# Hybrid conv/mLSTM step with a mixture of experts: the order of work at the first three expert slots

## The reference, cut to what matters

```python
gp = softmax(x @ w_rg + b_rg); gsel = argmax(gp)              # one group of 4
ep = softmax((x @ w_re + b_re)[group gsel]); top 2 of 4       # two experts in the group
combine = gp_sel * top2 / sum(top2)                           # weight of a token for an expert
g = x @ w_e_gate[e]; u = x @ w_e_up[e]                        # 1024 -> 256 each, 16 experts
act = silu(g) * u * combine[:, e]
out += act @ w_e_down[e]                                      # 256 -> 1024
x = x + gate2 * out; y = rms_norm(x)
```

## Time and profile before

| | |
|---|---|
| time, median of 3 runs | 734.84 us (733.2, 734.84, 737.28) |
| profiled execution, its time | 736.13 us |
| profiled execution, its span | 734.3 us |
| PE busy | 702.0 us (96%) |
| DVE busy | 542.5 us (74%) |
| ACT busy | 345.4 us (47%) |
| POOL busy | 212.8 us (29%) |
| moved by DMA | 149.10 MB |

### The profile page before, as it was taken

One profiled execution on the slowest core, in us unless ns is written; L12 is line 12 of the kernel. 1 busy time (PEld: TensorE's weight loads), 2 busy tenths in 40 slices (PEclk: granted clock), 3 DMA queues, 4 the chain that ended last, 5 costly groups with the idle time before them and its releaser, 6 DMA issues.

```text
span 734.3 us, 11162 instructions
## 1 busy us (share of the span) xinstructions
PE 702.0 (96%) x4432; PEld 612.8 (83%) x4432; DVE 542.5 (74%) x782; ACT 345.4 (47%) x457; POOL 212.8 (29%) x89
## 2 busy tenths in 40 slices
PE   5899999999999999999999999999889999998985
PEld 2499999999898898999999999887358888887863
DVE  3547999999858765865465574556599999988977
ACT  4552223432423443555276031124468888787634
POOL 4004321322200000000000000000129999989476
PEclk9999999999999999999999999999689999999998
DMA  9954145545624356441232534264958999989875
GB/s 332 375 163 143 59 173 173 173 173 174 206 92 77 66 122 128 44 133 58 62 118 75 162 115 144 114 258 162 420 182 335 398 402 409 416 326 398 312 252 197
DMA packets 75607, 149.10 MB, mean 203 GB/s; under 512 B 11302, under 2 KB 54626, under 8 KB 68836
## 3 DMA queue, kind: packets, MB, share of 16 engines
q1 hardware_dynamic: 61572, 125.28, 49.6%
q10 hardware_dynamic: 10096, 12.63, 4.7%
q0 software_dynamic: 3888, 10.49, 4.1%
HBM read 138.29 MB, written 20.05 MB: 216 GB/s over the span
## 4 chain that ended last, share of the span: by engine, by line
PE 60%; DVE 22%; DMA 6%; ACT 3%; issue 3%; POOL 2%; SPq 2%; POOLq 0%; DVEq 0%; ACTq 0%
PE psum L1009 19%; DVE psum L2045 14%; PE psum L1260 8%; PE psum L1302 7%; PE psum L515 4%; PE psum L514 4%; PE psum L520 4%; PE psum L944 3%; DMA down_raw<-in_w_e_down 2%; DMA w_more<-in_w_ada 2%; DMA xg<-h_d,slot_b 2%; SPq L807 1%; PE psum L1028 1%; PE psum L1137 1%; PE psum L1438 1%
## 5 line engine op out<-in xcount | busy, mean ns | idle before, releaser
L1009 PE MATMUL psum<-hh,w_h 128*128 128x320 f32 x608 | 144.9, 319 | 0.2 <-issue 0.2
L1009 PE MATMUL psum<-hh,w_l 128*128 128x320 f32 x608 | 138.8, 309 | 0.0
L1009 PE MATMUL psum<-hl,w_h 128*128 128x320 f32 x608 | 138.6, 309 | 0.0
L2045 DVE SCALAR_TENSOR_TENSOR psum<-conv,taps,psum 128x760 f32<-128x760 f32 x103 | 104.5, 1015 | 3.5
L1009 PEld LDWEIGHTS psum<-hh,w_h 128*128 128x128 f32 x608 | 100.2, 189 | 5.3 <-issue 3.1
L1009 PEld LDWEIGHTS psum<-hl,w_h 128*128 128x128 f32 x608 | 101.9, 188 | 0.0
L1009 PEld LDWEIGHTS psum<-hh,w_l 128*128 128x128 f32 x608 | 101.7, 188 | 0.0
L692 POOL TENSOR_TENSOR ob<-obh,toff 128x260 bf16<-128x260 f32 x1 | 2.0, 1995 | 333.5 <-DVE obh L600 333.5
L726 POOL TENSOR_TENSOR down_l<-down_raw,down_h 128x2048 fp32r<-128x2048 f32 x16 | 87.6, 5472 | 19.3 <-ACT down_h L1813 18.9
L2331 DVE TENSOR_TENSOR w_l<-w_raw,w_h 128x2048 fp32r<-128x2048 f32 x26 | 76.9, 2961 | 11.3 <-ACT w_h L1819 11.3
L936 POOL TENSOR_TENSOR w_l<-w_raw,w_h 128x2048 fp32r<-128x2048 f32 x9 | 41.7, 4638 | 144.0 <-ACT w_h L1494 144.0
(11 more groups left out here) (385 smaller groups left out, 1412.7 us busy)
## 6 DMA issues: line engine op xcount, KB each, us to landing
w_raw<-in_w_in SPq DMA_DIRECT2D x20, 1024.0 KB, 6.9
down_raw<-in_w_e_down SPq DMA_DIRECT2D x17, 1024.0 KB, 12.6
w_raw<-in_w_ada SPq DMA_DIRECT2D x16, 1024.0 KB, 9.2
w_raw<-in_w_e_gate SPq DMA_DIRECT2D x13, 1024.0 KB, 8.6
w_raw<-in_w_e_up SPq DMA_DIRECT2D x13, 1024.0 KB, 11.0
w_more<-in_w_ada SPq DMA_DIRECT2D x8, 1024.0 KB, 10.3
y_d<-yy ACTq DMA_DIRECT2D x15, 512.0 KB, 8.3
y_d<-in_x_sample SPq DMA_DIRECT2D x12, 512.0 KB, 8.1
```

Source lines behind the costliest of these rows:

```text
L1009: mm = pe.matmul(psum[:, p + q, 0:HALF], w, r[:, k, q * HALF:(q + 1) * HALF], start=(k == 0 and x == 0), stop=(k == KT - 1 and x == 2))
L2045: ins = dve.scalar_tensor_tensor(out=after, in0=src, scalar=w, in1=before, op0=MUL, op1=ADD)
```

## The change

Four edits, the first three at slots 0 and 1 alone.

1. PE, slot 0: the eight high products over the first four feature tiles (k 0 to 3) come ahead of `turn_x(1, 0, 1)`, and wait only for the first `x_lo`; the turns follow, then the other eight, which wait for the second `x_lo`. `with_high` gets a parameter `start`, so that the second half adds to the first.
2. PE, slot 1: `turn_x(0, 1, 2)` comes ahead of `turn_act(0)`.
3. ACT, slot 0: the copy of slot 1's gate weights (`w_hi(1, 1, 0, 0)`) comes ahead of the two `x_high` of slot 1, that of the up weights stays behind them.
4. ACT: one SiLU of a 128x1 column whose result nobody reads stands right behind the router's exponentials.

```diff
-    def with_high(pe, dst, terms):
+    def with_high(pe, dst, terms, start=True):
         for k, (lh, ll, rh) in enumerate(terms):
-            pe.matmul(dst, lh, rh, start=(k == 0), stop=False)
+            pe.matmul(dst, lh, rh, start=(start and k == 0), stop=False)
             pe.matmul(dst, ll, rh, start=False, stop=False)
...
         def slot(b, s, u, first=False, last=False):
-            if not first:
-                turn_act(b - 1, isinstance(b, int) and b == 1)
-            if not last:
-                turn_x(1 - s, u + s, b + 1)
+            second = isinstance(b, int) and b == 1
             wh, wl = w_h[:, 2 * s:2 * s + 2, :], low_of(b, s)
             both = lambda w, k: w[:, :, k * DE:(k + 1) * DE]
-            pe.wait_ge(x_lo, 2 * b + 2)
-            pe.wait_ge(e_hi, 2 * b + 2)
-            with_high(pe, psum[:, s, :], [(xh[:, s, k, :], xl[:, s, k, :], both(wh, k)) for k in range(KT)])
+            high = lambda ks: [(xh[:, s, k, :], xl[:, s, k, :], both(wh, k)) for k in ks]
+            if not first and not second:
+                turn_act(b - 1)
+            if not last and not first:
+                turn_x(1 - s, u + s, b + 1)
+            if second:
+                turn_act(b - 1, True)
+            if first:
+                pe.wait_ge(e_hi, 2)
+                pe.wait_ge(x_lo, 1)
+                with_high(pe, psum[:, s, :], high(range(KT // 2)))
+                turn_x(1 - s, u + s, b + 1)
+                pe.wait_ge(x_lo, 2)
+                with_high(pe, psum[:, s, :], high(range(KT // 2, KT)), start=False)
+            else:
+                pe.wait_ge(x_lo, 2 * b + 2)
+                pe.wait_ge(e_hi, 2 * b + 2)
+                with_high(pe, psum[:, s, :], high(range(KT)))
             pe.wait_ge(e_lo, 2 * b + 2)
...
             act.activation(src, src, ACT.Exp).then_inc(rt_exp, 1)
+        act.activation(rms[:, 31:32], ones[:, 0:1], ACT.Silu)
...
             if early > 0:
                 a_high(b - 1, early == 1)
+            if early == 0:
+                w_hi(1 - s, b + 1, u + s, 0)
             if not last:
                 for q in range(2):
                     x_high(1 - s, b + 1, q, early == 0)
...
             if not last:
-                for c in range(2):
+                for c in range(1 if early == 0 else 0, 2):
                     w_hi(1 - s, b + 1, u + s, c)
```

## The result

| | before | changed |
|---|---|---|
| median of 22 runs | 735.44 us (732.64 to 738.86) | 739.40 us (736.07 to 743.84) |
| ratio to before | | 1.0049, 95% interval 1.0033 to 1.0064 |
| profiled execution, time / span | 736.13 / 734.3 us | 736.32 / 734.5 us |

The change makes the kernel slower, by 4.0 us. The forecast was 0.5 us faster, and its range ended at 736.4. In two of the series a few executions of single kernels, the kernel before among them, took 872 to 1393 us; the ratios leave these out.

What follows compares the result with a forecast made beforehand. PE was taken to bound the expert slots, except at the change. It gains 1.01 us, gives back 0.73, and late waits make the end gain 0.5: 735.6 us profiled, 734.3 against the median, range 732.5 to 736.4.

Steps and rivals of the forecast that it cites:

- Edit 1: PE, slot 0: the pause inside the turns goes, gain 0.15 us; each half of the products is 1.87 us long.
- Edit 4: ACT's table load, moved from ahead of slot 0's SiLU: gains 0.04 us (bounds 0 and 0.07), costs nothing at its new place.
- drain: Rival: table switch adds about 1.38 us of drain on ACT; +0.5 us ahead of the slots, 734.8 us; chance 0.02.
- Edit 2, gain at slot 1: PE starts slot 1's products 1.01 us earlier: 0.15 + 0.04 + 0.82, slot 2's turns filling the wait for `act`.
- Given back at slot 2: PE waits 0.6 us for slot 1's `act`; of 1.01 us, 0.73 is given back, leaving PE 0.28 ahead.
- From there DVE's loop takes 9.24 per slot and PE's 9.32, so PE doesn't wait again.: From slot 2 on, DVE's loop is shorter than PE's, so PE has no further wait for it.
- The port of DVE and POOL: Slot 1: POOL's subtraction locks the shared port, so DVE's `w_l` takes 4.48 us, not 2.28, holding `act`.
- `xl` slips: Rival: slot 1's `xl` comes late on DVE, delaying slot 0's `act`; bound 2.2 us, net +0.7, 735.5 us; chance 0.08.
- What DMA makes of it: Earlier loads shorten late waits around slots 12 and 13; end gain between 0.28 and 1.4 us, taken as 0.5.
- the lead is lost: Rival: late slots are paced by DMA landing times that don't move; gain within 0.2 us, 734.8 us; chance 0.12.

Runs made afterwards that it cites:

- the three kernels with edit 2: Changed kernel with ACT evacuating slot 0's down product before slot 1's down copy; that plus padding; changed kernel plus eleven tiny ACT copies: 0.9992, 0.9997, 0.9985.
- ACT's new order, without and with padding: Changed kernel, ACT evacuating slot 0's down product before copying slot 1's down weights: 736.12 us; plus two tiny ACT copies at each of slots 2 to 4: 735.68 us.
- POOL's wait: Changed kernel with POOL's subtraction of slot 1's down weights waiting for DVE's copy of slot 2's up weights: 740.94 us, ratio 1.0067.
- ACT's order in the kernel before: Kernel before, with ACT at slot 1 evacuating slot 0's down product ahead of copying slot 1's down weights: 740.38 us, ratio 1.0059.
- eleven copies: Changed kernel with eleven one-column ACT copies between SiLU and the copy of the down weights at slot 1: 734.94 us, ratio 0.9985.

## Why the prediction was wrong, point by point

- *Edit 1.* Right in mechanism, smaller in size. ACT's and DVE's chain of slot 0 moved as worked out; SiLU of slot 0 starts 8.87 us behind the first transposes instead of 8.98, 0.11 earlier (forecast 0.19, within it the pause, 0.15). The pause went, but the two halves took 1.93 and 1.91 us, not 1.87 each, so that PE's slot 0 is shorter by 0.06 only. Without edit 2 the kernel is as fast as before. The prediction looked for no low clock in slot 0; three of the ten traces with edit 1 have one, at a price of 1.5 to 1.6 us.
- *Edit 4.* Right: the load cost nothing at its new place (g2row's copy waited 1.02 us for PE behind it), and no drain showed, as the trace of before had said.
- *Edit 2, gain at slot 1.* Right: slot 1's first product comes 546.19 - 536.11 = 10.08 behind the first transposes, against 550.37 - 539.27 = 11.10; 1.02 gained, forecast 1.01. That it fits so well is in part luck: 0.11 came up to slot 0's SiLU and 0.91 behind it, where 0.19 and 0.82 had been worked out.
- *Given back at slot 2.* Right in mechanism and size: PE waits 0.53 (forecast 0.6) for `act` of slot 1, and after this is 0.34 ahead, less 0.12 for the empty pipeline, 0.22 (forecast 0.28).
- *"From there DVE's loop takes 9.24 per slot and PE's 9.32, so PE doesn't wait again."* **This step failed.** It took a loop measured with one order of DVE and POOL for a constant. The same section had said that slot 1's `act` "hangs on slot 0's SiLU", and moves by 0.19; it had also moved the end of slot 1's gate and up products by 1.01 (the load that waits for the same `gu_done` as SiLU, from 556.13 to 555.12), and never asked what slot 1's SiLU and its follower on ACT, the copy of the down weights, then release. That copy went 0.9 us forward against DVE, POOL became ready first, and the next copy of DVE paid 5.1 us. The two rows that would have told are the two shown above from the trace before: 556.41 + 1.92 = 558.33 against 558.32. They are 0.01 us apart, and by the runs the order turns once this distance has moved by 0.03 to 0.29 us; edit 2 moved it by 0.90.
- *The port of DVE and POOL.* The prediction looked at one copy that POOL delays and did not ask for the next one. By the Trainium skill (SBUF — State Buffer, "SBUF: two separate sides") whoever starts first has the port for a whole instruction. The traces agree on the whole instruction. On who is first they show that the recorded start doesn't say it: DVE's copy starts ahead of POOL's subtraction in both kernels (0.59, and 0.58 before) and wins in one. What separates all traces is whether the instruction that POOL waits with has its last input by the time that DVE's begins.
- *The rivals.* The slower one, *`xl` slips*, had a chance of 0.08, a bound of 2.2 us and another mechanism; it did not occur. A swap of order at the port was in none of them. The price of DVE beside POOL was bounded by the 2.2 us that the trace of before showed; a whole subtraction, 4.6 us, stood in the same trace as what can lie ahead of a copy.
- *What DMA makes of it.* Open, and the traces rather speak for the rival *the lead is lost*. With the order mended, the three kernels with edit 2 stand at 0.9992, 0.9997 and 0.9985 of before, each interval holding 1; a gain of 0.5 us fits these as well as none. In the traces with ACT's new order, without and with padding, PE's late wait for `act` of slot 12 is gone (0.44 before), but that for the gathered rows behind it is 1.13 and 1.02 us instead of 0.69, and the next such wait 1.40 and 1.31 instead of 0.82. Counted from slot 0's first transposes, PE is 0.37 and 0.54 us ahead of the kernel before past the first of these waits, and 0.12 behind and 0.12 ahead past the second. That is one execution each. No version is shown to beat the kernel before.

How DVE and POOL are told apart inside the port isn't shown; the lead of ACT's copy is the condition that all runs obey, varied by PE's order, by ACT's order and by padding alone.

## What to carry to other kernels

When an edit moves one engine forward, list everything that it releases on the others, and look for pairs of instructions of DVE and POOL whose order could turn: the distance between the last input of the one and the start of the other is to be read in the trace, and a distance near zero is a risk of a whole instruction, not of that distance. A loop time from a trace holds only for the order that it ran in. And mending the order at one place must be checked at the next, since two edits here (POOL's wait, and ACT's order in the kernel before) left the copy for slot 2 short and made that for slot 3 long.

## What the runs showed of the hardware

- DVE's subtraction on 128x2048 takes 2.28 us alone and 7.37 when POOL's subtraction of 4.62 goes ahead of it; POOL's takes 6.19 when DVE's goes ahead. A gather in POOL's queue ahead of the subtraction (2.88 us) doesn't change who is next: it stood there in the long and the short case alike.
- The clock can be low in slot 0 too. In three of the traces with the changed order PE had waited 1.7 to 1.8 us for slot 0's gathered rows, and the first eight products ran at about the 1.2 GHz level (granted clock 0.51), 1.5 to 1.6 us longer than in the others. With eleven copies (stretch, length, busy, granted clock):

```profile
539.00:541.00 2.00, 1.48 (x18) 1.00 0.03 10
541.10:544.50 3.40, 3.31 (x8) 0.51 0.45 130
544.70:549.00 4.30, 4.30 (x25) 1.00 0.12 22
```

  The changed kernel's own trace, with a wait of 1.51 us, shows none of it, and neither does any of the order before, where that wait was 1.03 at most. It may hide part of what edit 1 gains. Whether the order has a part in it wasn't tried.
- Copies of one column on ACT, back to back, cost about 0.1 us each (1.12 for eleven).
